# Summing RWKV's decays by a product with a triangle of ones, behind the last pair scores

## What is computed

```python
w_log = -softplus(-(rwkv_w0 + tanh(xw) @ rwkv_w2)) - 0.5
decay = exp(-exp(w_log))                 # = exp(-exp(-0.5) * sigmoid(rwkv_w0 + ...))
a = sigmoid(rwkv_a0 + xa @ rwkv_a2)
g_r = sigmoid(xg) @ rwkv_g2
# S_t = S_{t-1} diag(decay_t) - (S_{t-1} kk_t)(kk_t * a_t)^T + v_t k_t^T ;  o_t = S_t r_t
```

## Time and profile before

| | |
|---|---|
| median of three runs | 1666.92 us (1666.18 to 1674.53) |
| profiled execution, its own time | 1674.23 us |
| its span | 1672.4 us, 23800 instructions |
| mean granted TensorE clock of the span | 0.987 |
| TensorE busy | 1640.9 us, 98% |
| VectorE busy | 861.7 us, 52% |
| ScalarE busy | 672.6 us, 40% |
| chain that ended last | TensorE 89%, VectorE 6%, ScalarE 4%, issue 1% |

### The profile page before, as it was taken

How to read it: one execution, slowest core, us unless ns; L and a number is a source line. 1 busy time by engine, 2 the same in 40 slices (tenths; PEclk the granted TensorE clock), 3 DMA queues, 4 the chain that set the end, 5 groups by cost and what they waited for, 6 DMA issues and landing times.

```text
span 1672.4 us, 23800 instructions
## 1 busy us (share of the span) xinstructions
PE 1640.9 (98%) x9522; PEld 1328.3 (79%) x9522; DVE 861.7 (52%) x1173; ACT 672.6 (40%) x1024; POOL 127.4 (8%) x126
## 2 busy tenths in 40 slices
PE   9999999999999999999999999999999999999997
PEld 6877778877777888888888878787987888888886
DVE  5733445552444566444433378678667554444333
ACT  6145565314656433323223355447343432333221
POOL 0001001100100020000000130000320200000000
PEclk9999999999999999999999999998799999999998
DMA  5412212332121223223333421220012222222331
GB/s 177 160 54 86 89 51 89 102 127 73 65 88 51 79 86 114 93 97 101 94 93 93 151 76 64 64 67 11 12 33 87 88 102 101 99 90 83 103 103 52
DMA packets 40751, 144.15 MB, mean 86 GB/s; under 512 B 4816, under 2 KB 4832, under 8 KB 40256
## 3 DMA queue, kind: packets, MB, share of 16 engines
q1 hardware_dynamic: 37296, 131.61, 24.0%
q0 software_dynamic: 2192, 8.87, 1.6%
q10 hardware_dynamic: 1152, 2.14, 0.4%
HBM read 140.50 MB, written 2.10 MB: 85 GB/s over the span
## 4 chain that ended last, share of the span: by engine, by line
PE 89%; DVE 6%; ACT 4%; issue 1%; DMA 0%; POOL 0%; DVEq 0%; SPq 0%; ACTq 0%; POOLq 0%
PE bank L498 26%; PE bank L500 25%; PE bank L499 25%; PE bank L480 2%; PE bank L486 2%; PE bank L1045 2%; PE bank L879 1%; PE bank L665 1%; PE bank L729 1%; PE bank L708 1%; DVE sb_w_low L1268 1%; ACT sb_w_high L2071 1%; PE bank L905 1%; DMA sb_x<-xT 0%; ACT sb_xg_high L2071 0%
## 5 line engine op out<-in xcount | busy, mean ns | idle before, releaser
L1268 DVE TENSOR_TENSOR sb_w_low<-sb_raw,sb_w_high 128x1024 fp32r<-128x1024 f32 (+1 forms) x253 | 312.7, 1236 | 365.2 <-ACT sb_w_high L2071 358.5
L498 PE MATMUL bank<-sb_xg_high,sb_w_high 128*128 128x512 f32 x1176 | 465.9, 396 | 3.3 <-DVE sb_w_low L1268 2.3
L500 PE MATMUL bank<-sb_xg_high,sb_w_low 128*128 128x512 f32 x1176 | 458.8, 390 | 0.0
L499 PE MATMUL bank<-sb_xg_low,sb_w_high 128*128 128x512 f32 x1176 | 458.5, 390 | 0.0
L2071 ACT ACTIVATE sb_w_high<-sb_raw 128x1024 fp32r<-128x1024 f32 (+1 forms) x253 | 263.3, 1041 | 347.3 <-PE bank L500 323.4
L498 PEld LDWEIGHTS bank<-sb_xg_high,sb_w_high 128*128 128x128 f32 x1176 | 221.1, 188 | 66.4 <-issue 16.7
L500 PEld LDWEIGHTS bank<-sb_xg_high,sb_w_low 128*128 128x128 f32 x1176 | 221.1, 188 | 47.2
L499 PEld LDWEIGHTS bank<-sb_xg_low,sb_w_high 128*128 128x128 f32 x1176 | 221.3, 188 | 44.3 <-issue 0.2
L500 PE MATMUL bank<-sb_h_high,sb_w_low 128*128 128x512 f32 x352 | 136.9, 389 | 0.0
L498 PE MATMUL bank<-sb_h_high,sb_w_high 128*128 128x512 f32 x352 | 136.9, 389 | 0.0
L499 PE MATMUL bank<-sb_h_low,sb_w_high 128*128 128x512 f32 x352 | 136.9, 389 | 0.0
(11 more groups left out here) (338 smaller groups left out, 1969.1 us busy)
## 6 DMA issues: line engine op xcount, KB each, us to landing
sb_raw<-w_ffn_in SPq DMA_DIRECT2D x88, 512.0 KB, 3.4
sb_raw<-w_ffn_out SPq DMA_DIRECT2D x32, 512.0 KB, 3.5
sb_raw<-w_tok SPq DMA_DIRECT2D x24, 512.0 KB, 3.7
sb_raw<-w_mix_f SPq DMA_DIRECT2D x18, 512.0 KB, 3.5
sb_raw<-w_rot SPq DMA_DIRECT2D x16, 512.0 KB, 3.6
sb_raw<-w_qk SPq DMA_DIRECT2D x16, 512.0 KB, 3.4
sb_raw<-w_out SPq DMA_DIRECT2D x16, 512.0 KB, 3.4
sb_raw<-w_ffn_out SPq DMA_DIRECT2D x16, 384.0 KB, 3.1
```

The lines of the kernel that those rows point to most:

```text
L498: e.matmul(out, w[0], v[0], start=first, stop=False)
L499: e.matmul(out, w[0], v[1], start=False, stop=False)
L500: return e.matmul(out, w[1], v[0], start=False, stop=last)
L1268: e.tensor_tensor(out, a, b, op).then_inc(*v.up(*signal))
```

## The change

The gate's products come first and alone. Sigma is made with tokens in the partitions: the low-rank product has `mixed` as the stationary side, and `rwkv_w0` is added by a second product with a first column of the identity and a row of the table (`rows`, now three). ScalarE takes the gate's sigmoids and key gains in step 6, then sigma's and the output gate's in step 7, with a dummy exp behind each. TensorE sums the sigmas by a product with `sums`, a 128 x 128 table with two triangles of ones, behind level 128's scores and ahead of the turned keys; the result is by features again and ScalarE reads it from PSUM in step 8. The scans and the idle products are gone. The pair masks are stored with the right halves alone, and the mixer table shrinks from 2176 to 1856 columns.

```diff
 
 
 N_SHARED = 128
-MIXER = {"same_head": (0, 128), "before": (128, 64), "upto": (192, 64), "pairs": (256, 7 * 128),
-         "pairs_ts": (1152, 64), "restart": (1216, 512), "chunk_pairs": (1728, 6 * 64), "chunk_ident": (2112, 64)}
-N_MIXER = 2176
+MIXER = {"same_head": (0, 128), "before": (128, 64), "upto": (192, 64), "pairs": (256, 7 * 64),
+         "pairs_ts": (704, 64), "restart": (768, 512), "chunk_pairs": (1280, 6 * 64), "chunk_ident": (1664, 64),
+         "sums": (1728, 128)}
+N_MIXER = 1856
 
 
 
 SHARED_BY = {}
 for _sem, _names in (
-        ("rwkv operands by T", "sigma in,a gate in,gate out,key norm,key turned,bonus in,tokA turned,tokB turned"),
+        ("rwkv operands by T", "sigma in,sigma summed,a gate in,gate out,key norm,key turned,bonus in,tokA turned,tokB turned"),
         ("rwkv operands by S", "rwkv tanh,rwkv sigmoid,sigma,a gate,g tok,key squares,key spread,rwkv exps,rwkv fades,bonus,tokA,tokB,"
                                "rwkv own,X preset,XT preset"),
-        ("rwkv operands by V", "key floored,key scaled,sigma summed,bI,bonus products,kI,rE,rwkv landed,rwkv mixed"),
+        ("rwkv operands by V", "key floored,key scaled,bI,bonus products,kI,rE,rwkv landed,rwkv mixed"),
         ("inverse by T", "AT product,X product,A_ak product,Gv product,M_rk product,M_rb product,W1 product,"
                          "W2T product,X step,XT step,Pm product"),
         ("inverse by V", "X made,AT,X,XT made,A_ak,M_rk,M_rb,W2T"),
...
@@ -352,14 +354,14 @@
 
     def pairs(self, m):
         n = LEVELS.index(m)
-        return self.table("pairs")[:, n * P:(n + 1) * P]
+        return self.table("pairs")[:, n * 64:(n + 1) * 64]
 
     def chunk_pairs(self, m):
         n = LEVELS.index(m) - 1
         return self.table("chunk_pairs")[:, n * CHUNK:(n + 1) * CHUNK]
 
     def pair_mask(self, m, n_tiles):
-        v = halves(self.pairs(m), m, True)
+        v = self.pairs(m).rearrange("p (n c) -> p n c", c=m)
         return v.unsqueeze(1).to_broadcast([P, n_tiles, v.shape[1], m])
 
...
@@ -931,8 +933,6 @@
                     before_last()
                     keep_busy(1)
                 scores(n)
-                if before_last and ORDER[n] == 64:
-                    keep_busy(2)
             if name == "gla":
                 fill(len(ORDER))
                 gram("AT", HEAD_PAIRS[0], m.bI, m.kkE)
...
@@ -999,11 +999,28 @@
                 transposes(i, [flat(m.key_sq)[:, blk(2 * t + f)] for t in range(TT)], "key turned", f)
 
         def low_rank_gates():
-            for what, r in (("sigma", slice(0, 64)), ("a gate", slice(64, 128))):
-                for f in range(2):
-                    i = take((what, f), (what, f))
-                    p.wait_ge(*of("rwkv tanh"))
-                    group(banks[i][:, :], [(m.lora[r, 0, blk(f)], m.mixed[r, 6, :])], what + " in", f)
+            for f in range(2):
+                i = take(("a gate", f), ("a gate", f))
+                p.wait_ge(*of("rwkv tanh"))
+                group(banks[i][:, :], [(m.lora[64:128, 0, blk(f)], m.mixed[64:128, 6, :])], "a gate in", f)
+
+        def token_sigmas():
+            first_row = mem.ident[:, 0:1].to_broadcast([P, P])
+            for half in range(2):
+                i = take(("sigma", half), ("sigma", half))
+                for j in range(2):
+                    group(banks[i][:, j * G:(j + 1) * G],
+                          [(m.mixed[0:64, 6, blk(2 * half + j)], m.lora[0:64, 0, :]), (first_row, m.rows[:, 2, :])],
+                          "sigma in", half)
+
+        def sum_sigmas():
+            out = [take(("cum", f), ("rwkv exps", f)) for f in range(2)]
+            p.wait_ge(*of("sigma", 1))
+            for f in range(2):
+                for t in range(TT):
+                    made = e.matmul(banks[out[f]][:, blk(t)], m.sigma_tok[:, t, blk(f)], mem.table("sums"), start=True,
+                                    stop=True)
+                made.then_inc(*p.up("sigma summed", f))
 
         def output_gate():
             for half in range(2):
...
@@ -1029,10 +1046,16 @@
                     p.mark("xg read", MIX_NORM)
             elif n == 6:
                 low_rank_gates()
+            elif n == 7:
+                token_sigmas()
             elif n == 9:
                 output_gate()
 
-        linear_attention("gla", fill_gla, turn_keys)
+        def before_last():
+            sum_sigmas()
+            turn_keys()
+
+        linear_attention("gla", fill_gla, before_last)
         inverse(m, gram, turn_values)
         p.mark("TensorE at", "recurrence")
         recurrence(m)
...
@@ -1811,12 +1834,6 @@
             v.wait_ge(*of("key norm"))
             ts(small[:, 176:192], bank("key norm")[:, 0:16], 1e-24, None, ALU.max, ALU.bypass, "key floored")
 
-        def sum_sigmas(n):
-            if n == 6:
-                for f in range(2):
-                    v.wait_ge(*of("sigma", f))
-                    scan(m.cum[:, f, :], m.sigma[:, f, :], "sigma summed", f)
-
         def operand_steps():
             by_chunk = lambda ap: ap.rearrange("p (n c) -> p n c", c=CHUNK)
             for f in range(2):
@@ -1824,11 +1841,11 @@
                 stt(kk[:, f, :], rk[:, f, :], mem.col("rwkv_k_k", f), bank("key turned", f)[:, :], ALU.mult, ALU.mult,
                     "key scaled", f)
                 out, keys, fades = (by_chunk(ap[:, f, :]) for ap in (m.kkE, kk, m.eB))
-                v.wait_ge(*of("rwkv fades"))
+                v.wait_ge(*of("rwkv fades", f))
                 tt(out[:, :, 1:], keys[:, :, 1:], fades[:, :, 0:CHUNK - 1], ALU.mult, *STEP)
                 ts(out[:, :, 0:1], keys[:, :, 0:1], 1.0, None, ALU.mult, ALU.bypass, *STEP)
                 v.wait_ge(*of("a gate", 1))
-                v.wait_ge(*of("rwkv exps"))
+                v.wait_ge(*of("rwkv exps", f))
                 tt(m.bI[:, f, :], kk[:, f, :], m.a_gate[:, f, :], ALU.mult, *STEP)
                 stt(m.bI[:, f, :], m.bI[:, f, :], -1.0, eI[:, f, :], ALU.mult, ALU.mult, "bI", f)
             first_triangles(m, 0)
...
@@ -2497,14 +2514,23 @@
             a.wait_ge(*of("key inverse"))
             act(heads(flat(m.key_sq)), small[:, 176:192].unsqueeze(2).to_broadcast([P, 16, 64]), "key spread")
 
-        def sigmoids():
+        def gate_sigmoids():
+            a.wait_ge(*of("xg read", MIX_NORM))
+            for f in range(2):
+                a.wait_ge(*of("a gate in", f))
+                act(m.a_gate[:, f, :], bank("a gate", f)[:, :], "a gate", f, func=ACT.Sigmoid,
+                    bias=mem.col("rwkv_a0", f))
+            key_gains()
+            act(small[:, 250:251], mem.ones[:, 0:1], *STEP, func=ACT.Exp)
+
+        def decay_sigmoids():
             a.wait_ge(*of("rwkv mixed", 7))
-            a.wait_ge(*of("xg read", MIX_NORM))
-            for what, out, bias in (("sigma", m.sigma, "rwkv_w0"), ("a gate", m.a_gate, "rwkv_a0")):
-                for f in range(2):
-                    a.wait_ge(*of(what + " in", f))
-                    act(out[:, f, :], bank(what, f)[:, :], what, f, func=ACT.Sigmoid, bias=mem.col(bias, f))
+            for half in range(2):
+                a.wait_ge(*of("sigma in", half))
+                act(m.sigma_tok[:, 2 * half:2 * half + 2, :], groups_of(bank("sigma", half)[:, :], G), "sigma", half,
+                    func=ACT.Sigmoid)
             act(m.mixed[:, 7, :], m.mixed[:, 7, :], "rwkv sigmoid", func=ACT.Sigmoid)
+            act(small[:, 250:251], mem.ones[:, 0:1], *STEP, func=ACT.Exp)
 
         def key_gains():
             a.wait_ge(*of("keys kept"))
@@ -2513,9 +2539,10 @@
                     bias=small[:, 108 + f:109 + f])
 
         def raise_decays():
-            a.wait_ge(*of("sigma summed", 1))
-            act(m.eB, m.cum, "rwkv fades", func=ACT.Exp, scale=-HALF_E)
-            act(m.rE, m.cum, "rwkv exps", func=ACT.Exp, scale=HALF_E)
+            for f in range(2):
+                a.wait_ge(*of("sigma summed", f))
+                act(m.eB[:, f, :], bank("cum", f)[:, :], "rwkv fades", f, func=ACT.Exp, scale=-HALF_E)
+                act(m.rE[:, f, :], bank("cum", f)[:, :], "rwkv exps", f, func=ACT.Exp, scale=HALF_E)
 
         def land_gate():
             for half in range(2):
@@ -2544,9 +2571,10 @@
                 if n in (2, 4):
                     next(projections)
             elif n == 6:
-                sigmoids()
+                gate_sigmoids()
             elif n == 7:
-                key_gains()
+                decay_sigmoids()
+            elif n == 8:
                 raise_decays()
             elif n == 9:
                 land_gate()
...
@@ -2890,8 +2918,9 @@
     row, col = r % CHUNK, np.arange(CHUNK)[None, :]
     put("before", (row < col).astype(f32))
     put("upto", (row <= col).astype(f32))
+    put("sums", ((r // CHUNK == c // CHUNK) & (r <= c)).astype(f32))
     pair = lambda m, s, t: ((s // (2 * m) == t // (2 * m)) & (s // m % 2 == 0) & (t // m % 2 == 1))
-    put("pairs", np.stack([pair(m, r, c) for m in LEVELS], 1).astype(f32))
```

(8 more changed lines are left out.)

## The result

| | before | after |
|---|---|---|
| median of 16 runs each, taken together | 1671.0 us | 1675.38 us |
| lowest and highest | 1665.61, 1674.57 | 1670.52, 1679.62 |
| profiled execution, its span | 1674.23, 1672.4 | 1676.64, 1674.8 |

What follows compares the result with a forecast made beforehand. The prediction took VectorE to set the end from 1143.4 to 1167.25 us, with ScalarE close beside it. Later far copies delay value products by 2.0 us, other terms 0: 1668.9 us on a median of 1666.92, range 1664.0 to 1677.5.

Steps and rivals of the forecast that it cites:

- So what VectorE saves it spends waiting for this factor: ScalarE's factor for level 256 (called level 128's) ends when it did before, so the scans' 2.6 us become waiting.
- Rival B: VectorE's gain comes through: 2.6 us less, 1664.3 us, with dense masks up to 4.9 less, 1662.0; chance 0.20.
- The exponentials ahead of the far copies: On ScalarE, four exponentials now stand ahead of level 128's far copies; level 256's far copies end 2.5 us later.
- The step that failed: On TensorE, level 256's scores start after two far copies and take 2.0 us; value products start 2.0 us later.
- The sign named for this: Value products would wait for ScalarE's last far copy, not for VectorE's bI.
- rival C: Slower: TensorE's clock stays halved until after level 256's scores; about +8 on top of 2.0, 1677 us; chance 0.17.
- Sigmas by tokens, 2.8 us, bounds 2.0 to 4.0: Four pairs of TensorE products making the sigmas: 2.8 us, almost all where TensorE stood idle, 0 to 0.3 us.
- Sums, 2.2 us at the full clock: TensorE's eight products that sum the sigmas: 3.4 us at half clock or 2.2 at full; cost 0 either way.
- Idle products behind level 64: 0: Removing TensorE's idle products behind level 64's scores costs 0 directly, since they filled a wait.
- Masks: 0: VectorE's masked copies with dense masks: bounds 0 and -2.3 us, taken as 0 because ScalarE covers both.
- The second half clock costs about 8 us: The later half-clock stretch, 17.1 us of nearly solid TensorE work, makes some executions about 8 us dearer.
- A's own range: The forecast case, ScalarE's second sigmoid-table visit eats the scans' gain: +2.0, 1668.9 us, range 1666 to 1672, chance 0.60.

Runs made afterwards that it cites:

- one table: Changed kernel with sigmoid computed through tanh, which shares exp's table, so all four table loads go: median 1668.29 us, ratio 1.0003 to before.
- two loads more: Kernel before with only a dummy sigmoid and a dummy exp added ahead of the key gains: ratio 1.0003 to before, value products at 28.40 us.
- idle products back: Changed kernel with the two idle products behind level 64's scores put back: ratio 1.0021 to before, value products at 28.91 us.
- one visit: Changed kernel with the tokens' sigmas moved into the gates' step, so two table loads fewer: median 1673.44 us, ratio 1.0022 to before.
- new order: Changed kernel, all four loads kept, far copies ahead of exponentials, presets last, no idle product left: median 1668.54 us, ratio 0.9991 to before.

## Why the prediction was right, and by what it was off

- *"So what VectorE saves it spends waiting for this factor"*: right, but for the level's name. The factor ends at 18.1 us, as worked out, and VectorE waits 1.95 us. Rival B, whose gain needed an earlier factor, fell with this.
- *The exponentials ahead of the far copies "and that is the cost"*: right. First far copy 20.84 (forecast 20.7), last one's end 27.31 (27.04). Loads alone on the kernel before reproduce it, and one table or another order takes it away. Of the 3.96 us this bounds 2.5: behind the last far copy values could have started at 27.45, before 24.98.
- **The step that failed**: *"Now TensorE starts level 256's scores when two far copies are done, 1165.0, has them out by 1167.0"*, and with it *"two ahead of level 256"* in the list of idle products that go. By these the scores would be out at 23.6 behind the landing; they were out at 26.0. I misread the diff: it takes away only the idle products behind level 64. The remaining one came first in that bank, 1.1 us, and behind the 3.69 us of standing still the clock fell, so that the scores took 3.60 us in the chain instead of 1.93. With them at the full clock, idle product included, the chain gives 1168.1, which the far copies cover; so the half clock is what stands uncovered, **1.5 us** (28.94 less 27.45). The sign named for this, value products that wait for the last far copy, did not come either: they follow the grams without a wait. The prediction's own times held the gap: at the full clock the first keys are turned at 1161.0 and the scores start at 1165.0. It did not ask what the clock does behind that, and against rival C it counted "some seven nearly unbroken microseconds of products" there. Without the idle product 28.42 remained and the clock fell too, so the idle product is not the cause of the fall. What is stays open. TensorE had stood still 1.91 us ahead of a fall at this place with two loads more, 2.82 with the idle products back, 3.69 here and 4.25 without any idle product; the clock stayed at 1.00 there behind 1.34 us (one table, one visit) and 1.83 (new order). But those kernels differ in more than this wait, and the run that was to fill it put its idle products on the path instead.
- *Rival C* had the mechanism (the clock returns only behind level 256's scores) but not the size: it came back with the output gate's products, not behind the values, and cost 1.5 us where C said 8. The clock of the stretch 1149 to 1163, which fell in before, stayed at 1.00 here; that was worth nothing, as VectorE or ScalarE set the end there in both kernels.
- *Sigmas by tokens, 2.8 us, bounds 2.0 to 4.0*: 5.0, outside. The width was halved and the time was not. Hidden, as said, though with less room: TensorE's idle time ahead of level 128's scores (level 64's in the prediction) was 1.31 us, not 3.8, and in the run with one visit it was on the path. *Sums, 2.2 us at the full clock*: 1.9.
- *Idle products behind level 64: 0*: right, by two runs. *Masks: 0*: right, density is not what makes these copies slow; what does was not tried.
- *The second half clock costs about 8 us*: 7.3 by the two executions above. *On the median of 1666.92*: a median of three was a poor base for a kernel whose executions fall apart so. That 1675.38 still lies between 1664.0 and 1677.5 is in part luck: A's own range, 1666 to 1672, misses it, and the upper end was put there for C, whose 8 us came out as 1.5. *"0.79 with the part of C"*: A and B alone are 0.80, so this sum is off by a little.

By these terms the stretch is 2.0 forecast, 0.5 more on ScalarE and 1.5 for the clock. The rest to 4.7, 0.7 us, is within the interval. One place to look for it: from the mixer's output (`sb_y_high`) to the end the profiled execution took 444.40 us, before 443.10. The three executions without the change have 443.0 to 443.1 there, seven of the eight with it 444.4 to 445.2, the kernel of one table 442.99. No run tells why.

## What to carry to other kernels

Work that is taken from the engine that sets the end is worth only the slack of the one next to it: 2.6 us left VectorE, and ScalarE, which had almost none, got two table loads. When a stage ends in copies that free banks, put these copies ahead of everything that is awaited less; on the changed kernel this order, with the idle product gone, gave back 3.4 of 3.96 us with every load in place. And read a diff for what stays as closely as for what goes.

## What the runs showed of the hardware

- A table load takes 1.28 us and little more: in the run with two loads more, the next activation starts 0.01 to 0.02 us behind each of the two added loads. The Trainium skill (ScalarE: Activation LUTs, "What ACT_TABLE_LOAD costs") adds a drain of about 1380 ns; no kernel here shows one.
- Products of 64 rows and of 128 rows in turn, 256 columns wide, took 0.63 us each of either kind, where those of 64 rows and 512 columns take 0.50 and those of 128 rows and 256 columns 0.50 in a row by themselves (four in 1.99 us).
- The clock can fall behind a wait and be back 3.4 us later: 1163.3 to 1166.7 in the changed kernel. With two loads more it was at 0.50 three times between 8.6 and 25.7 us behind the landing.
- 17.1 us at the half clock cost 7.3 us and not half of them, 8.55; what covers the rest was not looked into. That a kernel has this stretch in some executions and lacks it in others would fit the way its totals fall apart, but with one profile for each kernel it is not shown.
